# Four modulation rows moved from TensorE to VectorE ahead of the convolution, and two pairs of rows moved behind the attention scores, in a two-block transformer kernel on one core

## What is computed

```python
c_act = jax.nn.silu(c)
mod = c_act @ ada_w[l] + ada_b[l]
sh1, sc1, g1, sh2, sc2, g2 = jnp.split(mod, N_MOD, axis=-1)
h = rms_norm(x, mix_pre_g[l]) * (1.0 + sc1[:, None, :]) + sh1[:, None, :]
y = hybrid_mixer(h, w_in[l], conv_w[l], conv_b[l], conv_ln_g[l], conv_ln_b[l], w_out[l])
x = x + g1[:, None, :] * rms_norm(y, mix_post_g[l])
h = rms_norm(x, ffn_pre_g[l]) * (1.0 + sc2[:, None, :]) + sh2[:, None, :]
```

## Time and profile before

| | us |
|---|---|
| median of 3 runs | 2547.87 |
| lowest and highest | 2547.27, 2548.66 |
| the profiled execution, its own time | 2548.51 |
| its span | 2546.7 |

### The profile page before, as it was taken

How to read it: one execution, slowest core, us unless ns; L and a number is a source line. 1 busy time by engine, 2 the same in 40 slices (tenths; PEclk the granted TensorE clock), 3 DMA queues, 4 the chain that set the end, 5 groups by cost and what they waited for, 6 DMA issues and landing times.

```text
span 2546.7 us, 53371 instructions
## 1 busy us (share of the span) xinstructions
PE 2511.7 (99%) x21196; PEld 2435.4 (96%) x21196; DVE 1719.6 (68%) x2252; ACT 1282.8 (50%) x1827; POOL 61.1 (2%) x120
## 2 busy tenths in 40 slices
PE   7999999999999999999999999999999999999999
PEld 5778889999999999999999999999999999999999
DVE  5778977866666666558656655554866666677667
ACT  3378765644444444446545544444644444444445
POOL 0010000000000000000100000000000000000000
PEclk8999999999999999999999999999999999999999
DMA  9998778476666666565555555555455555555554
GB/s 399 395 403 340 289 254 303 157 231 224 225 223 228 229 224 192 182 196 157 181 164 165 160 186 180 188 182 184 146 185 193 179 189 196 185 187 187 185 182 141
DMA packets 136609, 547.36 MB, mean 215 GB/s; under 512 B 15312, under 2 KB 15568, under 8 KB 124080
## 3 DMA queue, kind: packets, MB, share of 16 engines
q1 hardware_dynamic: 126288, 474.08, 56.0%
q0 software_dynamic: 9760, 68.94, 7.2%
q10 hardware_dynamic: 448, 2.75, 0.3%
HBM read 543.59 MB, written 2.12 MB: 214 GB/s over the span
## 4 chain that ended last, share of the span: by engine, by line
PE 94%; DVE 2%; DMA 2%; ACT 2%; issue 0%; SPq 0%; DVEq 0%; ACTq 0%
PE bank L1994 20%; PE bank L1996 20%; PE bank L1995 20%; PE bank L2205 9%; PE bank L2207 8%; PE bank L2206 8%; DMA ada_pre<-in_ada_first 2%; PE bank L2018 1%; PE bank L2078 1%; PE bank L2080 1%; PE bank L2079 1%; PE bank L2145 1%; DMA raw<-in_w_in 1%; DVE w_lo L1173 1%; ACT w_hi L580 1%; PE bank L2163 0%
## 5 line engine op out<-in xcount | busy, mean ns | idle before, releaser
L1173 DVE TENSOR_TENSOR w_lo<-raw,w_hi 128x1024 fp32r<-128x1024 f32 x836 | 1014.0, 1223 | 620.6 <-ACT w_hi L580 619.0
L580 ACT ACTIVATE w_hi<-raw 128x1024 fp32r<-128x1024 f32 x836 | 874.5, 1057 | 783.9 <-PE bank L1996 447.4
L1994 PE MATMUL bank<-h_hi,w_hi 128*128 128x258 f32 (+1 forms) x2576 | 730.8, 284 | 2.0 <-DVE h_lo L1259 0.8
L1995 PE MATMUL bank<-h_lo,w_hi 128*128 128x258 f32 (+1 forms) x2576 | 727.2, 282 | 0.0
L1996 PE MATMUL bank<-h_hi,w_lo 128*128 128x258 f32 (+1 forms) x2576 | 727.1, 282 | 0.0
L1994 PEld LDWEIGHTS bank<-h_hi,w_hi 128*128 128x128 f32 x2576 | 485.1, 188 | 5.6 <-issue 3.0
L1995 PEld LDWEIGHTS bank<-h_lo,w_hi 128*128 128x128 f32 x2576 | 485.1, 188 | 0.6 <-issue 0.5
L1996 PEld LDWEIGHTS bank<-h_hi,w_lo 128*128 128x128 f32 x2576 | 485.1, 188 | 0.0
L2205 PE MATMUL bank<-hid_hi,w_hi 128*128 128x256 f32 x1280 | 353.9, 277 | 0.0
L2206 PE MATMUL bank<-hid_lo,w_hi 128*128 128x256 f32 x1280 | 353.7, 276 | 0.0
L2207 PE MATMUL bank<-hid_hi,w_lo 128*128 128x256 f32 x1280 | 353.7, 276 | 0.0
(11 more groups left out here) (280 smaller groups left out, 3484.5 us busy)
## 6 DMA issues: line engine op xcount, KB each, us to landing
raw<-in_w_in SPq DMA_DIRECT2D x208, 512.0 KB, 4.2
raw<-in_w_ffn_up SPq DMA_DIRECT2D x176, 512.0 KB, 4.2
ada_raw<-in_ada_w POOLq DMA_DIRECT2D x64, 1024.0 KB, 8.3
raw<-in_w_gate SPq DMA_DIRECT2D x88, 512.0 KB, 4.3
raw<-in_w_up SPq DMA_DIRECT2D x88, 512.0 KB, 4.2
raw<-in_w_down SPq DMA_DIRECT2D x88, 512.0 KB, 4.2
raw<-in_w_ffn_down SPq DMA_DIRECT2D x88, 512.0 KB, 4.4
ada_pre<-in_ada_first SPq DMA_DIRECT2D x32, 1024.0 KB, 11.2
```

Of the source, the lines that this page charges most:

```text
L580: act.activation(w_hi[:, slot], raw[:, slot], ACT.Copy).then_inc(hi_ready, 1)
L1173: dve.tensor_tensor(w_lo[:, slot], raw[:, slot], fp(w_hi[:, slot]), ALU.subtract).then_inc(lo_ready, 1)
L1994: pe.matmul(dst, wh, x_hi(kt), start=first and k == 0, stop=False)
L1995: pe.matmul(dst, wh, x_lo(kt), start=False, stop=False)
```

## The change

Rows 0, 1, 2 and 4 of part 2 become summed rows. VectorE takes rows 0 and 1 ahead of its work for g = 0, row 2 in g = 1 and row 4 in g = 3. TensorE's timed rows of part 2 are then 3 and 5 to 15: ahead of the halves of g = 3 to 7 and of n = 0 to 6 in body 0. `sum_rows` for part 2 stands ahead of n = 8 of body 0. In bodies 1 and 2 the pair of rows from ahead of n = 0 stands at n = 1, behind the first head's scores. The tables of the convolution are shifted a little. The rest of the diff keeps the counts of the semaphores right.

```diff
-ADA_HEADS = (tuple(range(10)), (0, 0, 4, 4, 9, 9), (0, 0, 4, 4, 9, 9), (5, 7, 9, 11))
+ADA_HEADS = (tuple(range(7)), (4, 4, 9, 9), (4, 4, 9, 9), (5, 7, 9, 11))
...
-SUMMED = [a for a in range(4 * KT) if KT < a < 2 * KT and a % 8 in (2, 5) or a == 2 * KT + 5 or a >= 2 * KT + 7]
+SUMMED = [a for a in range(4 * KT) if a in (0, 1, 2, 4) or KT < a < 2 * KT and a % 8 in (2, 5) or a == 2 * KT + 5 or a >= 2 * KT + 7]
...
-CONV_OPS = (0, 0, 0, 0, 1, 2, 3, 3, 3, 3, 4, 3, 3, 3, 4, 3, 3, 3, 2, 2, 3, 2, 1, 3, 2, 0, 2, 3,
+CONV_OPS = (0, 0, 0, 0, 1, 3, 3, 3, 3, 3, 4, 3, 3, 3, 3, 3, 2, 2, 2, 2, 4, 2, 2, 3, 2, 0, 2, 3,
...
@@ block.scalar, body 0
                     if pair is None and n == 10:
-                        act.wait_ge(ada_used, KT)
+                        act.wait_ge(acc_summed, 1)
                         copy_rows(2, B_N)
@@ block.vector
             taken = 0
+            early_row(True)
+            early_row()
             for g in range(OPEN):
                 dve.wait_ge(half_used, done.next())
                 if g % 2:
                     gated(OPEN_BANK[g], g // 2)
                 convert()
+                if g in (1, 3):
+                    early_row()
                 conv_ops(g)
@@ block.tensor, the opening
             for g in range(OPEN):
-                if g == 2:
+                if g == 3:
                     pe.wait_ge(ag_sig, 1)
-                if g >= 2:
+                if g >= 3:
                     ada_row(ada, B_N)
                     ada += 1
                 opened(g, 3)
@@ block.tensor, the bodies
+                    if body == 0 and n == 8:
+                        sum_rows(SUMMED_2, B_N)
...
                     if body:
                         attend1(n, v_ready)
+                    if body in (1, 2) and n == 1:
+                        for _ in range(2):
+                            ada_row(ada, 3)
+                            ada += 1
```

More of the change, by code:

```diff
@@ L54 @@
 ADA_ADDED = (7, 8, 10, 12, 14, 16, 18, 19, 20, 21)
-SUMMED = [a for a in range(4 * KT) if KT < a < 2 * KT and a % 8 in (2, 5) or a == 2 * KT + 5 or a >= 2 * KT + 7]
+SUMMED = [a for a in range(4 * KT) if a in (0, 1, 2, 4) or KT < a < 2 * KT and a % 8 in (2, 5) or a == 2 * KT + 5 or a >= 2 * KT + 7]
 TIMED = [a for a in range(4 * KT) if a not in SUMMED]
+FIRST = [min(a for a in TIMED if a // KT == part) for part in range(3)]
+SUMMED_2 = sum(a < KT for a in SUMMED)
 SUMMED_3 = sum(a < 2 * KT for a in SUMMED)
@@ L61 @@
 CONV_STEPS = 4 * DVE_TAPS + ACT_TAPS
-CONV_OPS = (0, 0, 0, 0, 1, 2, 3, 3, 3, 3, 4, 3, 3, 3, 4, 3, 3, 3, 2, 2, 3, 2, 1, 3, 2, 0, 2, 3,
+CONV_OPS = (0, 0, 0, 0, 1, 3, 3, 3, 3, 3, 4, 3, 3, 3, 3, 3, 2, 2, 2, 2, 4, 2, 2, 3, 2, 0, 2, 3,
             3, 3, 2, 2, 3, 2, 1, 3, 2, 0, 2, 3, 3, 3, 2, 2, 3, 2, 2, 2, 2, 0, 0, 0, 0, 0, 0, 0)
-CONV_UNITS = (0, 0, 0, 0, 2, 1, 1, 1, 1, 1, 1, 2, 1, 1, 2, 1, 1, 2, 0, 2, 0, 1, 1, 0, 0, 2, 1, 1,
+CONV_UNITS = (0, 0, 0, 0, 2, 1, 1, 1, 1, 2, 1, 1, 2, 1, 1, 1, 1, 1, 1, 1, 1, 1, 1, 0, 0, 2, 1, 1,
               1, 1, 1, 1, 1, 1, 1, 1, 0, 0, 2, 0, 2, 1, 1, 1, 1, 0, 1, 1, 0, 0, 0, 0, 0, 0, 0, 0)
@@ L802, in heads1 @@
                     if pair is None and n == 10:
-                        act.wait_ge(ada_used, KT)
+                        act.wait_ge(acc_summed, 1)
                         copy_rows(2, B_N)
                     if last and n == 1:
-                        act.wait_ge(acc_summed, 1)
+                        act.wait_ge(acc_summed, 2)
                         copy_rows(3, 3)
@@ L842, in _ @@
                 if n == 25:
-                    act.wait_ge(acc_summed, 2)
+                    act.wait_ge(acc_summed, 3)
                     act.wait_ge(mod_ready, 1)
@@ L1415, in early_row @@
                 if first:
-                    if summed:
-                        dve.wait_ge(acc_summed, 1)
+                    if a >= KT:
+                        dve.wait_ge(acc_summed, a // KT)
                     op = dve.tensor_scalar(acc[:, :], ada_raw[:, slot], cact[:, kt:kt + 1], None, ALU.mult)
@@ L1530, in _ @@
                     if n in ADA_HEADS_ADDED[body]:
-                        early_row(summed == 0)
+                        early_row(summed in (SUMMED_2, SUMMED_3))
                     conv_ops(OPEN + 12 * body + n)
@@ L1566, in _ @@
                 if n in ADA_ADDED:
-                    early_row(n == ADA_ADDED[0])
+                    early_row(summed == SUMMED_3)
                 if n == 10:
@@ L2012, in quarter, with ada_products @@
                      range(kt0 + 4 * q, kt0 + 4 * q + 4), cols.stop - cols.start, q == 0, q == n_kt // 4 - 1)
-            def ada_products(rows, slot, kt, b):
+            def ada_products(rows, slot, kt, b, first):
                 for g in range(4):
                     mm = pe.matmul(bank[32 * g:32 * g + 32, b, :], cact[:, kt:kt + 1].to_broadcast([128, 32]),
-                                   rows[:, slot, 512 * g:512 * g + 512], start=kt == 0, stop=kt == KT - 1 and b == B_N)
+                                   rows[:, slot, 512 * g:512 * g + 512], start=first, stop=False)
                 return mm
@@ L2026, in ada_row @@
                 pe.wait_ge(ada_loaded[slot], 16 * (a // ADA_RING + 1))
-                ada_products(ada_raw, slot, ADA_ROW[a][1], b).then_inc(ada_used, 1)
+                ada_products(ada_raw, slot, ADA_ROW[a][1], b, a in FIRST).then_inc(ada_used, 1)
             def turn_rows(n, b):
@@ L2209, in half_one, with sum_rows @@
                 halves.next()
-            def sum_rows(n):
+            def sum_rows(n, b):
                 pe.wait_ge(row_added, n)
                 for g in range(4):
-                    mm = pe.matmul(bank[32 * g:32 * g + 32, 3, :], ones[:, 0:32], acc[:, 512 * g:512 * g + 512],
+                    mm = pe.matmul(bank[32 * g:32 * g + 32, b, :], ones[:, 0:32], acc[:, 512 * g:512 * g + 512],
                                    start=False, stop=True)
@@ L2230, in _ @@
                     if body == 3 and n == 0:
-                        sum_rows(SUMMED_3)
+                        sum_rows(SUMMED_3, 3)
                     if body == 3 and n == 3:
@@ L2259, in _ @@
                 if n == 24:
-                    sum_rows(SUMMED_4)
+                    sum_rows(SUMMED_4, 3)
                 if n == 27:
```

## The result

| | before | after |
|---|---|---|
| median of 6 runs each, us | 2549.14 | 2559.77 |
| lowest and highest, us | 2547.27, 2550.61 | 2555.68, 2560.31 |
| profiled execution, own time, us | 2548.51 | 2558.76 |
| its span, us | 2546.7 | 2557.0 |

The ratio is 1.0038, with a 95% interval from 1.0026 to 1.0049: slower, by 6.6 to 12.5 us. The sign, and in the opening the place and the mechanism, are those of the forecast. The size is not: 2559.77 lies 1.3 us above the range.

What follows compares the result with a forecast made beforehand. TensorE was taken to bound the kernel: -3.6 saved, +3.0 and +5.7 for two load waits, +0.5 for row 7, +1.2 for the clock, +6.8 us in all, giving 2554.7 us against 2547.87; range 2550.8 to 2558.5.

Steps and rivals of the forecast that it cites:

- Bound, savings: TensorE, busy 99% of the span, sets the time; four rows leave it and one sum comes, saving 3.6 us.
- VectorE's work at nothing: VectorE's added 8.3 us of row additions in the opening cost nothing, hidden in its idle stretches.
- First wait, 3.0: TensorE, done at 139.9 us, waits 3.0 us for row 3's load, landing at 142.9; between 1.8 and 5.5.
- The short waits of the rivals: Rival: both opening waits near their lower ends, no fall of the clock, +1.4 to +3.9 us; chance 0.20.
- Second wait, row 5 at 152.5: Row 5's load, released by VectorE's row 2 addition, lands at 152.5; TensorE waits 5.7 us, between 3.2 and 7.2.
- about 1 us later: VectorE's split of half 28, ahead of row 2's addition, moves about 1 us later than its 140.6 to 141.8.
- 4 to 7 us: Sign to look for: a TensorE wait of this length for `ada_raw` near 147 to 153 us.
- The clock, 1.2: Behind the wait for row 5, a 3.4 us stretch at half the clock costs 1.2 us, between 0 and 1.7.
- The rival with the longer stretch: Rival: three 3.4 us stretches at half the clock, or late rows in the bodies, +8.5 to +11 us; chance 0.12.
- Row 7, 0.5: Row 7's load, whose slot VectorE frees with row 4 in g = 3, makes TensorE wait 0.5 us, between 0 and 2.
- The pairs at 0: Moving the pairs in bodies 1 and 2 behind the scores costs 0, with 2 us a body as far end.
- 0.7 us to spare, no wait: In body 2 the scores come at 252.2 us, after ScalarE's copy ends at 251.5, so they wait for nothing.

Runs made afterwards that it cites:

- e7: Kernel after, but VectorE adds rows 0 to 3 and TensorE begins with row 4 ahead of g = 5, sum at n = 9: 2553.11 us, ratio 1.0018.
- e4: Kernel after plus four idle matmuls, read by nobody, ahead of TensorE's wait for row 5: 2557.62 us, ratio 1.0035.
- e4b: Kernel after plus idle matmuls ahead of both waits, four before row 3 and seven before row 5: 2557.76 us, ratio 1.0033.
- e2: Kernel after with the pairs of bodies 1 and 2 put back ahead of n = 0: 2557.70 us, ratio 1.0037.
- e3: Kernel after with VectorE's addition of row 2 one step earlier, ahead of the split of half 28: 2556.21 us, ratio 1.0031.
- e1: Kernel before with only the pairs of bodies 1 and 2 moved behind the scores: 2552.22 us, ratio 1.0013.
- f4: Kernel before with only the pairs moved behind the scores, run again for a second profile: 2551.36 us, ratio 1.0005.
- f3: Kernel before with the pairs behind the scores and the rows of n = 4 moved to n = 5: 2549.24 us, ratio 0.9998.
- e5: Kernel after, but VectorE adds only rows 0 and 1; TensorE begins with row 2 ahead of g = 3, sum at n = 9: 2552.52 us, ratio 1.0015.
- e6: Kernel after, but VectorE adds rows 0 to 2; TensorE begins with row 3 ahead of g = 4, sum at n = 9: 2551.22 us, ratio 1.0013.

## Why the prediction was half right

- **Bound, savings.** Right. TensorE sets the time and loses three rows' worth; no run measures the 3.6 us alone, but the sum below closes with them. Nothing behind the changed bodies gave anything back: from part 4's turn on it is 2123.7 us before and 2123.4 after.
- **VectorE's work at nothing.** Right for after, where TensorE waits for no split; e7 has one such wait, 0.64 us. What counts is what stands *ahead* of an addition in its list, as the forecast had it.
- **First wait, 3.0.** Measured 3.94. Row 3 was issued at 133.70 in before's time (134.53 - 0.83), as predicted (133.9), but took 10.2 us instead of 9.0. The forecast added 3.0 as a term of its own. e4 and e4b show that no such term can be added on top of row 5: row 5's issue hangs on VectorE's list, not on TensorE, so a longer first wait makes the second shorter by as much. The forecast's two terms were at least worked out that way, as one end at 152.5, so their sum stands. The short waits of the rivals were not: 1.8 + 3.2 adds a second wait that was counted from a first one of 3.0, and with landings at 141.7 and 150.0 both together are 6.2.
- **Second wait, row 5 at 152.5.** Right mechanism, 1.5 us short: 153.97 in before's time. The split of half 28 stood at 142.65 where "about 1 us later" had put it at 141.6, so the issue came at 146.43 instead of 145.3; the load took 7.5 instead of 7.2. The wait itself was 3.27 us, not 5.7 and not the "4 to 7 us" that was to show it: the forecast had no fall of the clock behind the first wait, and that fall used up, at no cost, a part of the second.
- **The clock, 1.2, "between 0 and 1.7".** This is the term of the opening that failed. It was sized from one row of 3.4 us. The stretch behind the second wait was 6.8 us long with TensorE at work in it, and cost 2.85 (6.78 - 3.93). The rival with the longer stretch had the size, but I gave it 0.12. That the falls are not always there (e2) makes this a term with a spread of 2.8 us from run to run.
- **Row 7, 0.5.** No wait, and not for the fall of the clock: e2 and e4b, at full clock there, had none either. Row 7's load took 5.9 us in after and 6.2 in e2. In e3, where row 5 is sooner, the wait appears, 1.40.
- **In sum** the opening came to 6.8 + 1.5 + 1.65 - 0.5 = 9.45 us, measured 9.36.
- **The pairs at 0, "with 2 us a body as the far end".** Wrong by e1, f4 and f3. The step that failed: "issued later they find less queued, at 5.5 to 8.7 us each". They were issued 3 us later and took 7.1 and 10.3 (e1), so the second landed at 265.18, with TensorE due there at 264.2. Since the earlier trace rows showed its predecessor landing just when TensorE got to it, with no reserve, zero was the lower end of this term, not its middle. For ScalarE's copy the "0.7 us to spare, no wait" held in after; e5 and e6 waited 0.56 and 1.35 us for it in body 1.

Both misses have the same sign, and the range was built around a sum that had neither. By the median the kernel lost 10.6 us: 9.4 in the profiled opening and the rest from the pairs and from what a run scatters; how the last 1 us divides between these two stays open. The medians would fit 6.6 for the loads, some 2 for the clock (after +10.6, e4b_fill_both +8.3) and some 1.7 for the pairs, but their intervals are too wide to show it.

## What to carry to other kernels

When a slot of a load ring passes from one engine to another, write down the new releaser and everything that stands ahead of it in its engine's list. Here a row that had landed held its slot for 4.8 us more behind a split that waited for a load which the ring itself was delaying. Take for a late load the end that it lands at, not a sum of waits along the way: earlier waits only use up the same time. And where the trace shows a load landing as its user arrives, price a later issue at its full delay, with a fall of the clock as a possible extra of about 3 us.

## What the runs showed of the hardware

- **The length of a wait does not tell whether the clock falls.** A stretch at the lower level, 1.2 GHz, followed waits of 3.94 and 3.27 us (after), 4.20 (e2_rows), 2.20 (f4_pairs_again, 0.62 from 268 to 272 us), 1.84 (e7_first4, 0.58 from 158 to 162) and 1.35 (e6_first3, 0.62 from 210 to 214); it stayed at 1.00 behind waits of 3.61 (e2_rows), 1.98 (e3_row2_early), 1.26 (e6_first3) and 1.02 (e1_pairs). The stretches at 1.2 GHz were 6.8 to 6.9 us long in after and in e2_rows, and some 3.4 in e4_fill, e3_row2_early, e6_first3, e7_first4 and f4_pairs_again. The Trainium skill, page "TensorE: Matmul & The Clock Gate", section "HAM oscillation — how this bites in real kernels", says that a TensorE which waits for transfers between its bursts is put back to half its clock each time; the rows agree for the first five of these waits, all for loads, and e2's second wait speaks against a rule without exception.
- **A fall costs only when TensorE is what is late.** The one behind row 3 lasted 6.9 us in after and cost nothing beside e4b_fill_both, where it was absent (row 5 used 27.5 and 27.6 us behind row 0's issue); the one behind row 5, as long, cost 2.8.
- **TensorE kept busy with matmuls that nobody reads holds the clock** (1.00 over 17 us in e4b_fill_both), but does not bring the awaited load sooner.
- **Two busy queues share the bytes unevenly.** With 1.09 MB on q0 beside it, q1 moved 0.57 MB in 4 us where it had moved 1.22, and the load of a half took 11.5 us instead of 9.5.
